# Single transposes and value products placed between the tile products of an attention head

## The chip, the cores and the metric

The kernel runs on one core of one Trainium2 chip. The metric is the time of one execution in microseconds (us) on the device. TensorE (PE) does the matrix products and the transposes, ScalarE (ACT) and VectorE (DVE) the elementwise work, and DMA queues move data between HBM and SBUF. A matrix product needs its weights loaded first; the profile shows these loads as an engine row of their own, PEld.

## The reference

One step of a two-layer encoder trunk on 512 prompt rows and 8 x 16 sample rows, 640 rows in all, model width 1024:

```
for each layer:
  q, k, v (differential attention) | q, k, v (sliding window) | two gates = x @ w_in
  for each of 8 heads, both maps m:  p_m = softmax(q_m k_m^T)        # chunk-causal
      a = p_0 - lambda * p_1 ;  o = a @ v                            # prompt rows: 4 blocks of 128
      samples: the same over 512 cached rows and the 16 new ones
      o = o * rsqrt(mean(o^2) + eps) * g
  x = LayerNorm(ALPHA * x + (sig(g_a) * (A @ w_a) + sig(g_b) * (B @ w_b)) @ w_o)
  x = LayerNorm(ALPHA * x + relu(x @ w_up)^2 @ w_down)
```

## The kernel before

All engines run programs written out by hand, in order, tied by semaphores. The large products are made in a split form: each operand is a high and a low part, and a block of 128 input rows (k = 0 to 7) takes three PE products, high by high, high by low, low by high (L602, L603, L604 in `feature_tile`). One product has 128x128 weights and moves 320 columns. A tile (128 output rows, one half of the 640 columns) is 8 x 3 = 24 such products. Below they are called tile products and numbered 0 to 23 within a tile.

Head h of the attention runs among the tiles that make q and k of head h+1. PE's order in `head(l, h)` is:

1. tile(0,0), q of the next head, first half. At k = 6 stands `mean_squares` of the head before (L873).
2. `unit_product(3)` of the head before (L867), then the scores of the samples (L745, L754, L755).
3. tile(0,1), then the masks (L822) and the scores of units 0 to 2 (L842). A unit is a block of 128 prompt rows; unit i sees i+1 blocks of keys. The masks overwrite the banks of the sample scores, so the first four wait until ACT has taken the exponentials of sample group 0, and the last two for those of group 1 (L1322, semaphore `dec_exp`).
4. `output_transposes` of the head before (L762, four), then tile(1,0), k of the next head, with `dec_transposes` of sample groups 0 and 1 (L777, five each) at k = 2 and k = 5. Both groups write the same place in PSUM: group 1 waits until ACT has copied group 0 out (L1330, `dec_t_copied`).
5. `dec_products` (L787 for the new rows, L795 for the cached ones), `last_score` (L831, L833), `unit_transpose((0, 1))` (L856, three).
6. tile(1,1), with `dec_map_sum` (L805) at k = 4 and `unit_product((0, 1))` and `unit_transpose((2,))` at k = 5. Behind it `unit_product((2,))` and `unit_transpose((3,))`. A unit's product waits until ACT has copied its transposed probabilities out of PSUM (L1314, `unit_t_copied`).

A product of two full-precision operands (L867, L787, L805, L873, L745, L795) is two PE instructions, a transpose (L762, L777, L856, L1013) is one. L795 works in strips: the weights are 32 columns wide and four strips of the array run together.

ACT's order at the end of a head is: `unit_copy(1)`, `head_swap` (L1256, four), `unit_copy(2)`, the square `d_sq` (L1443, which `mean_squares` multiplies), and `high(1)` (L1229), which makes the high part of a weight chunk. DVE then makes the low part (`low(1)`, L2113), and behind that in its queue stands `dec_mean_squares` (L2181). ACT's next head begins with `dec_rsqrts` (L1343, L1345), which waits for L2181; behind it stand `head_swap` (L1256), `output_squares` (L1350) and `dec_exps` (L1322). DVE stands between the last two: L2186 and L2188 after the squares, then the maxima of the sample scores (L2227).

In the last head of a layer gate tiles stand in place of the next head's tiles. `last_head_end` begins with a tile whose banks ACT must have copied out in `gate_copy(1)` (L1373, `gate_copied`); in front of that copy stand `unit_copy(1)` and `a_high(3)` (L1388) in ACT's queue.

Outside the heads the change touches `first_tiles` (transposes of the last block of rows, L1013, which wait for DVE's L2628), and ACT's `branch_pair`.

Of the kernel before, what the change touches and what calls it, by code (L numbers as in the profile page):

```python
# [25 lines left out]
P = 128  # L26
# [6 lines left out]
RT = ROWS // P  # L33
# [3 lines left out]
HEADS = 8  # L37
# [3 lines left out]
BANK = 512  # L41
# [70 lines left out]
def build(nc, x_rows, x_cols, k_cache, v_cache, swa_kc, swa_vc, swa_k_keep, swa_v_keep, weights, cols,  # L112
# [3 lines left out]
    with ctx:  # L116
# [470 lines left out]
        def _(pe):  # L587
            mm = nc.tensor.matmul

            def feature_tile(s, n, hi, lo, which, part=None, between=None, slot=None, order=None):  # L590
                slot = s if slot is None else slot
                if order is None:
                    order = [(half, k) for half in ((0, 1) if part is None else (part,)) for k in range(KT)]
                if part != 1:
                    pe.wait_ge(w_ready[s], n + 1)
                for half, k in order:
                    out = PS[:, bank_of(which, half), 0:HALF]
                    c = slice(half * HALF, (half + 1) * HALF)
                    if between and (half, k) in between:
                        between[half, k]()  # L600
                    wh, wl = w_hi[slot][:, k * P:(k + 1) * P], w_lo[slot][:, k * P:(k + 1) * P]
                    mm(out, wh, hi[:, k, c], start=(k == 0), stop=False)  # L602
                    mm(out, wh, lo[:, k, c], start=False, stop=False)  # L603
                    last = mm(out, wl, hi[:, k, c], start=False, stop=(k == KT - 1))  # L604
                    if k == KT - 1:
                        last.then_inc((chunk_half_done if half == 0 else chunk_done)[s], 1)

            def x_blocks():
# [147 lines left out]

            def output_transposes(l, h, bank):

                n = l * HEADS + h
                pe.wait_ge(o_n_ready, n + 1)  # L760
                for i in range(4):
                    last = nc.tensor.transpose(PS[:, bank, i * P:(i + 1) * P], o_n[:, i, :], ident[:])  # L762
                last.then_inc(o_t_ready, 1)

            def dec_transposes(l, h, g):
                n = l * HEADS + h
                pe.wait_ge(dec_exp, 2 * n + g + 1)
                if g == 0:

                    pe.wait_ge(unit_t_copied, 3 * n)  # L770
                else:
                    pe.wait_ge(dec_t_copied, 2 * n + 1)
                for t in range(5):
                    if (g, t) == (0, 4):

                        pe.wait_ge(a_done, n)
                    last = nc.tensor.transpose(flat[:, 6 * BANK + t * P:6 * BANK + (t + 1) * P],  # L777
                                               d_p[:, g, t * P:(t + 1) * P], ident[:])
                last.then_inc(dec_t_ready, 1)

            def dec_products(l, h):

                n = l * HEADS + h
                pe.wait_ge(unit_exp, 4 * n + 2)
                for g in range(2):
                    pe.wait_ge(dec_t_copied, 2 * n + g + 1)
                    mm(PS[:, g, 0:P], d_pt[:, g, 4, :], rows[:, RT - 1, bass.ts(h, P)], start=True, stop=False,  # L787
                       skip_group_check=True)
                pe.wait_ge(vc_loaded, 16 * (n + 1))
                for g in range(2):  # L790
                    for t in range(4):
                        for b in range(4):
                            rows_of = slice(32 * b, 32 * (b + 1))
                            e = slice((4 * g + b) * P, (4 * g + b + 1) * P)
                            last = mm(PS[rows_of, g, 0:P], d_pt[:, g, t, rows_of], vc[:, t, e],  # L795
                                      start=False, stop=(t == 3), skip_group_check=True)
                    last.then_inc(dec_pv, 1)

            def dec_map_sum(l, h):

                n = l * HEADS + h
                pe.wait_ge(dec_o_copied, 2 * n + 2)
                pe.wait_ge(dec_sel_ready, n + 1)
                for g in range(2):
                    last = mm(PS[:, 0, g * 64:(g + 1) * 64], d_o[:, g, :], sel_r[:, g, :], start=True, stop=True)  # L805
                last.then_inc(dec_ot_ready, 1)

# [37 lines left out]

            def unit_transpose(l, h, units):
                n = l * HEADS + h
                pe.wait_ge(unit_probs, 4 * n + units[-1] + 1)
                if units[0] == 0:
                    pe.wait_ge(dec_t_copied, 2 * n + 2)  # L850
                else:
                    pe.wait_ge(unit_t_copied, 3 * n + units[0] - 1)
                at_col = 0
                for i in units:
                    for j in range(i + 1):
                        last = nc.tensor.transpose(PS[:, 6, at_col:at_col + P],  # L856
                                                   u_a_of[i][:, j * P:(j + 1) * P], ident[:])
                        at_col += P
                last.then_inc(unit_t_ready, 1)

            def unit_product(l, h, units):
                n = l * HEADS + h
                pe.wait_ge(unit_t_copied, 3 * n + max(units[-1], 1))
                for i in units:
                    for j in range(i + 1):
                        t = (j if i == 0 else 1 + j) if i < 2 else j
                        last = mm(PS[:, 7, i * P:(i + 1) * P], u_at[max(i - 1, 0) % 2][:, t * P:(t + 1) * P],  # L867
                                  rows[:, j, bass.ts(h, P)], start=(j == 0), stop=(j == i))
                last.then_inc(unit_pv, 1)

            def mean_squares(n):
                pe.wait_ge(dec_sq_ready, n + 1)
                mm(PS[:, 1, 0:P], ones[:], d_sq[:], start=True, stop=True).then_inc(dec_ms_ready, 1)  # L873

            def head(l, h, p, first, more, uses):

                n = l * HEADS + h

                def tile(is_k, half, between=None):
                    if more:  # L880
                        head_tile(l, h + 1, is_k, half, between)
                    else:
                        early_gate(l, is_k, half, between)

                tile(0, 0, None if first else {(0, 6): lambda: mean_squares(n - 1)})
                if not first:
                    unit_product(l, h - 1, (3,))
                else:
                    for r in range(RT):
# [12 lines left out]
                unit_score(l, h, p, (2,))  # L902
                if not first:
                    output_transposes(l, h - 1, 7)
                tile(1, 0, {(0, 2): lambda: dec_transposes(l, h, 0), (0, 5): lambda: dec_transposes(l, h, 1)})
                dec_products(l, h)
                last_score(l, h, p)
                unit_transpose(l, h, (0, 1))
                tile(1, 1, {(1, 4): lambda: dec_map_sum(l, h),
                            (1, 5): lambda: (unit_product(l, h, (0, 1)), unit_transpose(l, h, (2,)))})  # L910
                unit_product(l, h, (2,))
                unit_transpose(l, h, (3,))

            def last_head_end(l):
                early_gate(l, 2, 0, {(0, 6): lambda: mean_squares(l * HEADS + HEADS - 1)})
                unit_product(l, HEADS - 1, (3,))
                early_gate(l, 2, 1)
# [103 lines left out]
            def first_tiles(l, which, n):  # L1021

                group = l * GROUPS + 4 if which else l * GROUPS
                for half in range(2):
# [8 lines left out]
                    if half == 0:  # L1033
                        for r in range(3, RT):
                            pe.wait_ge(row_evacuated[r], group)
                    feature_tile(1, n, xt_hi, xt_lo, 1, half, slot=NEXT[1],
                                 between={(0, 3): lambda: x_transposes(l, which, 4, 0),
                                          (0, 5): lambda: x_transposes(l, which, 4, 1)})

# [25 lines left out]
            for l in range(DEPTH):  # L1065
# [11 lines left out]
                for u in range(FF_PAIRS):  # L1077
# [140 lines left out]
        def _(act):  # L1218
# [173 lines left out]
            def head(l, h, p, first, more, uses):  # L1392
# [43 lines left out]
                else:  # L1436
# [51 lines left out]
            def branch_pair(l, u):  # L1488
# [1701 lines left out]
```

## Time and profile before

| what | us |
|---|---|
| median of three runs | 2154.99 (2154.5 to 2155.03) |
| the profiled execution, its own time | 2154.7 |
| its span, first to last instruction | 2152.9 |
| PE busy | 2142.3 |
| PEld busy | 1961.0 |
| DVE busy | 1470.4 |
| ACT busy | 1182.9 |

PE is pipelined: the record of a tile product lasts 0.31 us, but products start 0.147 us apart. A busy PE therefore says little; the distances between starts do. The granted TensorE clock is 0.999 of full speed, which is the upper level, 2.4 GHz.

### The profile page before, as it was taken

The numbers are of one execution on the slowest core, as the hardware profiler recorded it, in microseconds if no ns is written. First come the engines' busy times: TensorE is split into PE (matmuls) and PEld (weight loads), VectorE is DVE, ScalarE is ACT, GpSimd is POOL, SyncE is SP. The second block draws the span as 40 slices with busy tenths as digits, with TensorE's granted clock in tenths as the row PEclk, the third lists the DMA queues.
The fourth block names the chain that finished last, engine by engine and source line by source line (L and its number), as shares of the span: only waits on it lengthen the run. The fifth ranks groups of instructions, "written<-read, shape, count | busy, mean of one in ns | idle before, by whom it ended". The sixth has DMA issues, their size and how long they took to land.

```text
span 2152.9 us, 38502 instructions
## 1 busy us (share of the span) xinstructions
PE 2142.3 (100%) x15174; PEld 1961.0 (91%) x15174; DVE 1470.4 (68%) x2420; ACT 1182.9 (55%) x2513; POOL 0.2 (0%) x4
## 2 busy tenths in 40 slices
PE   9999999999999999999999999999999999999998
PEld 8998889999989898989889888899999898989897
DVE  6757777776979373636667577786768793646466
ACT  4457776686535362626234677766865262627261
POOL 0000000000000000000000000000000000000000
PEclk9999999999999999999999999999999999999999
DMA  5367562531351222222333765525113412222231
GB/s 183 104 252 257 206 227 89 156 110 51 97 173 40 92 85 79 89 69 89 108 108 103 273 247 201 203 87 178 70 60 104 156 52 86 89 69 89 75 111 69
DMA packets 68162, 268.19 MB, mean 125 GB/s; under 512 B 10984, under 2 KB 12648, under 8 KB 61296
## 3 DMA queue, kind: packets, MB, share of 16 engines
q1 hardware_dynamic: 43136, 152.75, 20.9%
q10 hardware_dynamic: 24848, 112.99, 14.8%
q8 instruction: 121, 1.98, 0.4%
q14 instruction: 57, 0.47, 0.1%
HBM read 236.35 MB, written 25.95 MB: 122 GB/s over the span
## 4 chain that ended last, share of the span: by engine, by line
PE 97%; DVE 2%; issue 0%; ACT 0%; DMA 0%; DVEq 0%; ACTq 0%
PE PS L706 10%; PE PS L705 10%; PE PS L704 10%; PE PS L636 9%; PE PS L634 9%; PE PS L635 9%; PE PS L602 9%; PE PS L603 9%; PE PS L604 9%; PE PS L867 2%; PE PS L745 1%; PE PS L795 1%; PE PS L842 1%; PE PS L978 1%; PE PS L856 1%; PE PS L958 1%
## 5 line engine op out<-in xcount | busy, mean ns | idle before, releaser
L2113 DVE TENSOR_TENSOR w_lo<-w_raw,w_hi 128x1024 fp32r<-128x1024 f32 x178 | 216.0, 1223 | 243.3 <-ACT w_hi L1229 236.1
L602 PE MATMUL PS<-xt_hi,w_hi 128*128 128x320 f32 x1184 | 380.7, 322 | 0.0
L604 PE MATMUL PS<-xt_hi,w_lo 128*128 128x320 f32 x1184 | 365.7, 309 | 0.0
L603 PE MATMUL PS<-xt_lo,w_hi 128*128 128x320 f32 x1184 | 365.5, 309 | 0.0
L1229 ACT ACTIVATE w_hi<-w_raw 128x1024 fp32r<-128x1024 f32 x178 | 186.6, 1059 | 304.6 <-PE PS L706 284.2
L704 PE MATMUL PS<-w_hi,act_a_hi 128*128 128x512 f32 x800 | 312.2, 390 | 0.0
L706 PE MATMUL PS<-w_hi,act_a_lo 128*128 128x512 f32 x800 | 311.4, 389 | 0.0
L705 PE MATMUL PS<-w_lo,act_a_hi 128*128 128x512 f32 x800 | 311.4, 389 | 0.0
L602 PEld LDWEIGHTS PS<-xt_hi,w_hi 128*128 128x128 f32 x1184 | 222.7, 188 | 3.0 <-issue 1.4
L603 PEld LDWEIGHTS PS<-xt_lo,w_hi 128*128 128x128 f32 x1184 | 223.0, 188 | 0.1
L604 PEld LDWEIGHTS PS<-xt_hi,w_lo 128*128 128x128 f32 x1184 | 222.2, 188 | 0.0
L1256 ACT ACTIVATE rope_s<-PS 32x320 f32<-32x320 f32 x352 | 151.0, 429 | 55.5 <-DVE z_all L2104 27.9
L706 PEld LDWEIGHTS PS<-w_hi,act_a_lo 128*128 128x128 f32 x800 | 150.1, 188 | 31.3
L704 PEld LDWEIGHTS PS<-w_hi,act_a_hi 128*128 128x128 f32 x800 | 150.2, 188 | 30.9 <-issue 0.5
L705 PEld LDWEIGHTS PS<-w_lo,act_a_hi 128*128 128x128 f32 x800 | 150.2, 188 | 30.7
L2730 DVE TENSOR_TENSOR part_lo<-w_raw,part_hi 128x512 fp32r<-128x512 f32 x144 | 98.0, 688 | 56.8 <-ACT part_hi L1733 53.8
L1733 ACT ACTIVATE w_hi<-w_raw 128x512 fp32r<-128x512 f32 x130 | 78.6, 623 | 61.1 <-PE PS L706 48.8
L1733 ACT ACTIVATE part_hi<-w_raw 128x512 fp32r<-128x512 f32 x144 | 88.4, 623 | 30.2 <-DVE w_raw L2716 29.1
L634 PE MATMUL PS<-t_hi,part_hi 128*128 128x320 f32 x328 | 101.4, 309 | 0.0
L635 PE MATMUL PS<-t_lo,part_hi 128*128 128x320 f32 x328 | 101.4, 309 | 0.0
L636 PE MATMUL PS<-t_hi,part_lo 128*128 128x320 f32 x328 | 101.4, 309 | 0.0
L1764 ACT ACTIVATE PS<-PS 128x320 f32<-128x320 f32 x144 | 61.0, 424 | 70.4 <-PE PS L636 70.1
(342 smaller groups left out, 4794.2 us busy)
## 6 DMA issues: line engine op xcount, KB each, us to landing
w_raw<-in_weights SPq DMA_DIRECT2D x274, 512.0 KB, 3.5
kc<-in_k_cache ACTq DMA_DIRECT2D x32, 1024.0 KB, 8.0
vc<-in_v_cache ACTq DMA_DIRECT2D x16, 2048.0 KB, 8.9
gates_kept<-a_t ACTq DMA_DIRECT2D x8, 640.0 KB, 6.7
k_out<-k_t ACTq DMA_DIRECT2D x16, 320.0 KB, 2.4
v_out<-rows ACTq DMA_DIRECT2D x2, 2560.0 KB, 17.4
mix_a<-a_t ACTq DMA_DIRECT2D x2, 2560.0 KB, 12.6
rope_c<-gates_kept ACTq DMA_DIRECT2D x10, 320.0 KB, 3.1
```

Of the source, the lines that this page charges most:

```text
L602: mm(out, wh, hi[:, k, c], start=(k == 0), stop=False)
L603: mm(out, wh, lo[:, k, c], start=False, stop=False)
L604: last = mm(out, wl, hi[:, k, c], start=False, stop=(k == KT - 1))
L634: mm(up_bank(x), wh, moving[0][:, k], start=first and k == 0, stop=False, skip_group_check=True)
L635: mm(up_bank(x), wh, moving[1][:, k], start=False, stop=False, skip_group_check=True)
L636: last = mm(up_bank(x), wl, moving[0][:, k], start=False, stop=(k == KH - 1), skip_group_check=True)
L704: mm(out, xh, wh, start=(k == 0), stop=False)
L705: mm(out, xh, wl, start=False, stop=False)
L706: last = mm(out, xl, wh, start=False, stop=(k == KT - 1))
L1229: fn(w_hi[slot][:], raw[:, j, :], ACT.Copy).then_inc(w_hi_made[s], 1)
L1733: fn(parts_of(part)[0][part_place(n, o)][:], part_source(part, n, o), ACT.Copy) .then_inc(part_hi_made if o < 5 else w_hi_made[o - 5], 1)
L2113: v.tensor_tensor(w_lo[slot][:], raw[:, raw_of(s, n)[0], :], w_hi[slot][:].bitcast(F32), ALU.subtract)\
```

## The change

In the heads, groups of transposes and 128-column products are taken apart. A helper `spread(half, first, count, one)` puts one of them in front of each of `count` tile products in a row, beginning with number `first`. The new-row products of the samples become strips like the cached ones. ACT takes `d_sq` before `unit_copy(2)`. In `branch_pair`, for u = 0, `up_seed(2)` comes before the high part number 3. In `first_tiles` the transposes move from k = 3 and 5 to k = 4 and 6.

```
     if between and (half, k, 0) in between: between[half, k, 0]()
     mm(out, wh, hi[:, k, c], ...)          # likewise (half, k, 1), (half, k, 2) before the next two
+def spread(half, first, count, one):
+    return {(half, (first + x) // 3, (first + x) % 3): (lambda x=x: one(x)) for x in range(count)}
...
 def dec_products(l, h):
     pe.wait_ge(unit_exp, 4 * n + 2)
+    pe.wait_ge(vc_loaded, 16 * (n + 1))
     for g in range(2):
         pe.wait_ge(dec_t_copied, 2 * n + g + 1)
-        mm(PS[:, g, 0:P], d_pt[:, g, 4, :], rows[:, RT - 1, bass.ts(h, P)], start=True, stop=False,
-           skip_group_check=True)
-    pe.wait_ge(vc_loaded, 16 * (n + 1))
-    for g in range(2):
-        for t in range(4):
+        for t in range(5):
             for b in range(4):
...
+                values = vc[:, t, e] if t < 4 else rows[:, RT - 1, bass.ts(h, P)]
+                last = mm(PS[rows_of, g, 0:P], d_pt[:, g, t, rows_of], values,
+                          start=(t == 0), stop=(t == 4), skip_group_check=True)
...
+def head_end(l, h):
+    return {**spread(0, 0, 3, lambda x: unit_product(l, h, 2, x)),
+            **spread(0, 8, 4, lambda x: unit_transpose(l, h, 3, x)),
+            (0, 6): lambda: mean_squares(l * HEADS + h),
+            **spread(0, 20, 4, lambda x: unit_product(l, h, 3, x))}
 def head(l, h, p, first, more, uses):
-    tile(0, 0, None if first else {(0, 6): lambda: mean_squares(n - 1)})
-    if not first:
-        unit_product(l, h - 1, (3,))
-    else:
+    tile(0, 0, None if first else head_end(l, h - 1))
+    if first:
...
-    if not first:
-        output_transposes(l, h - 1, 7)
-    tile(1, 0, {(0, 2): lambda: dec_transposes(l, h, 0), (0, 5): lambda: dec_transposes(l, h, 1)})
+    tile(1, 0, {**({} if first else spread(0, 0, 4, lambda i: output_transpose(l, h - 1, 7, i))),
+                **spread(0, 6, 5, lambda t: dec_transpose(l, h, 0, t)),
+                **spread(0, 16, 5, lambda t: dec_transpose(l, h, 1, t))})
     dec_products(l, h)
     last_score(l, h, p)
-    unit_transpose(l, h, (0, 1))
-    tile(1, 1, {(1, 4): lambda: dec_map_sum(l, h),
-                (1, 5): lambda: (unit_product(l, h, (0, 1)), unit_transpose(l, h, (2,)))})
-    unit_product(l, h, (2,))
-    unit_transpose(l, h, (3,))
+    tile(1, 1, {**spread(1, 0, 3, lambda x: unit_transpose(l, h, 1, x)),
+                **spread(1, 12, 2, lambda g: dec_map_sum(l, h, g)),
+                **spread(1, 15, 3, lambda x: unit_product(l, h, 1, x)),
+                **spread(1, 18, 3, lambda x: unit_transpose(l, h, 2, x))})
 def last_head_end(l):
-    early_gate(l, 2, 0, {(0, 6): lambda: mean_squares(l * HEADS + HEADS - 1)})
-    unit_product(l, HEADS - 1, (3,))
+    early_gate(l, 2, 0, head_end(l, HEADS - 1))
     early_gate(l, 2, 1)
...
-                 between={(0, 3): lambda: x_transposes(l, which, 4, 0),
-                          (0, 5): lambda: x_transposes(l, which, 4, 1)})
+                 between={(0, 4): lambda: x_transposes(l, which, 4, 0),
+                          (0, 6): lambda: x_transposes(l, which, 4, 1)})
...
-                 between={(0, 3): lambda: output_transposes(l, HEADS - 1, 2)})
+                 between=spread(0, 9, 4, lambda i: output_transpose(l, HEADS - 1, 2, i)))
 # ACT, end of head(l, h)
-    unit_copy(l, h, 2)
     act.wait_ge(dec_summed, n + 1)
     fn(d_sq[:], d_out[:], ACT.Square).then_inc(dec_sq_ready, 1)
+    unit_copy(l, h, 2)
     high(1, nth(l, AT_HEADS, 2) + h)
 # ACT, branch_pair(l, u)
-    if not last:
+    if 0 < u < FF_PAIRS - 1:
         part_highs(l, BRANCH, u + 1, (3,))
     up_seed(l, BRANCH, u, 2)
+    if u == 0:
+        part_highs(l, BRANCH, u + 1, (3,))
```

The waits inside the taken-apart functions stay with the first piece: the first piece of a group waits for what the group waited for.

## Rows read from the trace of the kernel before

**Rows 1.** The page: the chain that ended last, shares of the span by engine.
```profile
PE 97%; DVE 2%; issue 0%; ACT 0%; DMA 0%; DVEq 0%; ACTq 0%
```

**Rows 2.** Busy time of PE, PEld, DVE, ACT in one head, layer 0, head 3.
```profile
212.22:239.94 27.72, 27.72 (x262) 24.31 (x261) 21.15 (x51) 20.37 (x53) 0.00 (x0) 1.00 0.56 202
```

**Rows 3.** Timeline (start, length), PE: tile products 1 and 23; transposes; `mean_squares`.
```profile
214.99 0.31 PE L603 MATMUL PS<-xt_lo,w_hi 128*128 128x320 f32 x1
...
218.22 0.31 PE L604 MATMUL PS<-xt_hi,w_lo 128*128 128x320 f32 x1
...
221.51 0.71 PE L777 MATMUL PS<-ident,d_p 128*128 128x128 f32 x5
...
222.21 0.31 PE L603 MATMUL PS<-xt_lo,w_hi 128*128 128x320 f32 x1
...
237.86 0.38 PE L873 MATMUL PS<-d_sq,ones 128*128 128x128 f32 x2
...
238.23 0.30 PE L603 MATMUL PS<-xt_lo,w_hi 128*128 128x320 f32 x1
```

**Rows 4.** Timeline, weight loads (PEld) behind a group of transposes.
```profile
318.47 0.19 PEld L602 LDWEIGHTS PS<-xt_hi,w_hi 128*128 128x128 f32 x1
318.58 0.19 PEld L603 LDWEIGHTS PS<-xt_lo,w_hi 128*128 128x128 f32 x1
```

**Rows 5.** Timeline, PE: into the strips, from a tile product and from L787.
```profile
129.23 0.31 PE L604 MATMUL PS<-xt_hi,w_lo 128*128 128x320 f32 x1
129.47 0.64 PE L745 MATMUL PS<-kc,z_all 128*32 128x512 f32 x4
...
142.10 0.60 PE L787 MATMUL PS<-rows,d_pt 128*128 128x128 f32 x4
142.64 1.95 PE L795 MATMUL PS<-vc,d_pt 128*32 128x128 f32 x64
144.52 1.13 PE L831 MATMUL PS<-k_t,q_t 64*128 64x512 f32 x4
```

**Rows 6.** Timeline, all engines: transposes of samples, ACT's copies out.
```profile
223.38 0.71 PE L777 MATMUL PS<-ident,d_p 128*128 128x128 f32 x5
...
224.13 0.71 ACT L1330 ACTIVATE d_pt<-PS 128x640 f32<-128x640 f32 x1 [0.25 <-PE PS L777]
```

**Rows 7.** Timeline, ACT: `unit_copy(1)` of head 3.
```profile
233.00 0.49 ACT L1314 ACTIVATE u_at<-PS 128x384 f32<-128x384 f32 x1
```

**Rows 8.** Timeline, the chain from `high(1)` through DVE to the masks.
```profile
236.78 1.05 ACT L1229 ACTIVATE w_hi<-w_raw 128x1024 fp32r<-128x1024 f32 x1
...
237.94 1.22 DVE L2113 TENSOR_TENSOR w_lo<-w_raw,w_hi 128x1024 fp32r<-128x1024 f32 x1
239.07 0.28 DVE L2181 TENSOR_SCALAR d_ms<-PS 128x128 f32<-128x128 f32 x1
...
239.39 0.31 ACT L1343 ACTIVATE d_rs<-d_ms 128x128 f32<-128x128 f32 x1 [1.56 <-DVE d_ms L2181]
...
217.93 0.20 ACT L1322 ACTIVATION_READ_ACCUMULATOR d_p<-PS,small 128x1 f32 x1
...
218.37 0.35 PE L822 MATMUL PS<-mask_cols 128*128 128x64 bf16 x6
```

**Rows 9.** Timeline, end of the last head of layer 0, ACT and PE.
```profile
344.47 0.46 ACT L1388 ACTIVATE aq_hi<-a_t 128x320 fp32r<-128x320 f32 x1
345.40 0.70 ACT L1373 ACTIVATE rope_s<-PS 128x640 f32<-128x640 f32 x1 [0.46 <-PE PS L604]
...
346.22 0.39 PE L602 MATMUL PS<-xt_hi,w_hi 128*128 128x320 f32 x1
```

**Rows 10.** Waits of PE's queue (L856 over the run; two in the timeline).
```profile
  DVE u_a L2175: 0.7, 3
...
1082.48 0.20 PEld L1013 LDWEIGHTS PS<-ident,rows 128*128 128x128 f32 x2 [0.35 <-DVE rows L2628]
...
386.65 0.19 PEld L634 LDWEIGHTS PS<-ta_hi,w_hi 128*128 128x128 f32 x1 [0.20 <-issue]
```

More of the change, by code:

```diff
@@ L601, in feature_tile @@
                     wh, wl = w_hi[slot][:, k * P:(k + 1) * P], w_lo[slot][:, k * P:(k + 1) * P]
+                    if between and (half, k, 0) in between:
+                        between[half, k, 0]()
                     mm(out, wh, hi[:, k, c], start=(k == 0), stop=False)
+                    if between and (half, k, 1) in between:
+                        between[half, k, 1]()
                     mm(out, wh, lo[:, k, c], start=False, stop=False)
+                    if between and (half, k, 2) in between:
+                        between[half, k, 2]()
                     last = mm(out, wl, hi[:, k, c], start=False, stop=(k == KT - 1))
@@ L755, in dec_new_scores, with output_transpose, dec_transpose @@
                     mm(new, m_own_dec[:, g, :], m_negnew, start=False, stop=True).then_inc(dec_scores, 1)
-            def output_transposes(l, h, bank):
+            def output_transpose(l, h, bank, i):
                 n = l * HEADS + h
[L760 to L765, printed above, removed]
-                n = l * HEADS + h
-                pe.wait_ge(dec_exp, 2 * n + g + 1)
-                if g == 0:
-                    pe.wait_ge(unit_t_copied, 3 * n)
-                else:
[L772 to L779, printed above, removed]
+                if i == 0:
+                    pe.wait_ge(o_n_ready, n + 1)
+                last = nc.tensor.transpose(PS[:, bank, i * P:(i + 1) * P], o_n[:, i, :], ident[:])
+                if i == 3:
+                    last.then_inc(o_t_ready, 1)
+            def dec_transpose(l, h, g, t):
+                n = l * HEADS + h
+                if t == 0:
+                    pe.wait_ge(dec_exp, 2 * n + g + 1)
+                    if g == 0:
+                        pe.wait_ge(unit_t_copied, 3 * n)
+                    else:
+                        pe.wait_ge(dec_t_copied, 2 * n + 1)
+                if (g, t) == (0, 4):
+                    pe.wait_ge(a_done, n)
+                last = nc.tensor.transpose(flat[:, 6 * BANK + t * P:6 * BANK + (t + 1) * P],
+                                           d_p[:, g, t * P:(t + 1) * P], ident[:])
+                if t == 4:
+                    last.then_inc(dec_t_ready, 1)
             def dec_products(l, h):
@@ L794, in dec_products, with dec_map_sum @@
                             e = slice((4 * g + b) * P, (4 * g + b + 1) * P)
-                            last = mm(PS[rows_of, g, 0:P], d_pt[:, g, t, rows_of], vc[:, t, e],
-                                      start=False, stop=(t == 3), skip_group_check=True)
+                            values = vc[:, t, e] if t < 4 else rows[:, RT - 1, bass.ts(h, P)]
+                            last = mm(PS[rows_of, g, 0:P], d_pt[:, g, t, rows_of], values,
+                                      start=(t == 0), stop=(t == 4), skip_group_check=True)
                     last.then_inc(dec_pv, 1)
-            def dec_map_sum(l, h):
+            def dec_map_sum(l, h, g):
                 n = l * HEADS + h
[L802 to L806, printed above, removed]
+                if g == 0:
+                    pe.wait_ge(dec_o_copied, 2 * n + 2)
+                    pe.wait_ge(dec_sel_ready, n + 1)
+                last = mm(PS[:, 0, g * 64:(g + 1) * 64], d_o[:, g, :], sel_r[:, g, :], start=True, stop=True)
+                if g == 1:
+                    last.then_inc(dec_ot_ready, 1)
             def unit_at(i, m):
@@ L844, in unit_score, with unit_transpose @@
                 last.then_inc(unit_scores, 1)
-            def unit_transpose(l, h, units):
+            def unit_transpose(l, h, last_unit, x):
                 n = l * HEADS + h
[L848 to L859, printed above, removed]
@@ L861, in unit_product @@
-            def unit_product(l, h, units):
-                n = l * HEADS + h
[L863 to L869, printed above, removed]
+                i, j = ((0, 0), (1, 0), (1, 1))[x] if last_unit == 1 else (last_unit, x)
@@ new lines, in unit_transpose @@
+                if x == 0:
+                    pe.wait_ge(unit_probs, 4 * n + last_unit + 1)
+                    if last_unit == 1:
+                        pe.wait_ge(dec_t_copied, 2 * n + 2)
+                    else:
+                        pe.wait_ge(unit_t_copied, 3 * n + last_unit - 1)
+                last = nc.tensor.transpose(PS[:, 6, x * P:(x + 1) * P], u_a_of[i][:, j * P:(j + 1) * P], ident[:])
+                if (i, j) == (last_unit, last_unit):
+                    last.then_inc(unit_t_ready, 1)
@@ new lines, in unit_product @@
+            def unit_product(l, h, last_unit, x):
+                n = l * HEADS + h
+                i, j = ((0, 0), (1, 0), (1, 1))[x] if last_unit == 1 else (last_unit, x)
+                if x == 0:
+                    pe.wait_ge(unit_t_copied, 3 * n + last_unit)
+                last = mm(PS[:, 7, i * P:(i + 1) * P], u_at[(last_unit - 1) % 2][:, x * P:(x + 1) * P],
+                          rows[:, j, bass.ts(h, P)], start=(j == 0), stop=(j == i))
+                if (i, j) == (last_unit, last_unit):
+                    last.then_inc(unit_pv, 1)
@@ L873, in mean_squares @@
                 mm(PS[:, 1, 0:P], ones[:], d_sq[:], start=True, stop=True).then_inc(dec_ms_ready, 1)
+            def head_end(l, h):
[3 more added lines that the diff above has]
+                        **spread(0, 20, 4, lambda x: unit_product(l, h, 3, x))}
             def head(l, h, p, first, more, uses):
-                n = l * HEADS + h
                 def tile(is_k, half, between=None):
@@ L883, in tile @@
                         early_gate(l, is_k, half, between)
-                tile(0, 0, None if first else {(0, 6): lambda: mean_squares(n - 1)})
-                if not first:
-                    unit_product(l, h - 1, (3,))
-                else:
+                tile(0, 0, None if first else head_end(l, h - 1))
+                if first:
                     for r in range(RT):
```

## Prediction

> **What bounds the kernel.** I read the page first, then a table of one head by engine, then the timeline of PE, and last ACT and DVE beside it. The chain that ended last is 97% PE [rows 1]. In head 3, 27.72 us long, PE is never idle, while ACT and DVE have some 7 us each to spare [rows 2]. So a change pays if it takes time out of PE's own sequence, and costs if PE must wait where it now does not. Head 3's row stands for five of that view: heads 1 to 5 of layer 0 are equally long to 0.01 us, which says that no chance wait falls in them. Since records overlap, I read distances between starts. Tile products 1 and 23 start at 214.99 and 218.22: 3.23 / 22 = 0.147 us each [rows 3].
>
> **What a transpose costs, in a group and alone.** From the first of five transposes (221.51) to the tile product after next (222.21) there are 0.70 us; less one tile product, 0.553 / 5 = 0.111 us each. For `mean_squares`, two instructions, it is 238.23 - 237.86 = 0.37, less 0.147: 0.112 each [rows 3]. The cost is the same for two and for five, so there is no price per group that taking groups apart could save or add. The reason is in the weight loads. Behind a transpose the load for L602 starts at 318.47 and the next at 318.58 [rows 4]: a load takes 0.11 us and begins when the product before it begins. A lone transpose hides its own load under the 0.147 us before it, but the load of the tile product behind it still starts with the transpose and takes 0.11. I take 0.110 us alone, as in a group. The bounds: 0.107 to 0.114, since starts are rounded and tile products behind a group run up to 0.01 us closer. Some 44 instructions a head are moved: 44 x 16 x 0.003 = 2 us either way, taken as 0.
>
> The Trainium skill (TensorE: Matmul & The Clock Gate, Part 2) says that PE pulls a weight load ahead of a running product into the background buffer. The trace agrees as far as one load, not two. Were the follower's load hidden as well, the sum would be the rival "faster" below.
>
> **Strips.** L787 to L795 takes 142.64 - 142.10 = 0.54, and 0.147 before it from the last tile product. The 64 strips take 144.52 - 142.64 = 1.88, with some 0.20 to leave; so four strips take about 0.11. Afterwards: 0.24 from a tile product into strips (129.47 - 129.23) and 16 strips more, 0.44 [rows 5]. 0.69 becomes 0.68: nothing. The number of changes between strips and the full array stays the same; `unit_product(3)` before L745 is equally even.
>
> **What is moved past a wait.** Here is the cost. A transpose must be copied out by ACT before its product, and the distance between the two has shrunk. The path: the last of five transposes starts at 223.38 + 4 x 0.109 = 223.82, ACT's copy at 224.13, 0.31 later, and lasts 0.71 [rows 6]. A signal takes about 0.05: DVE's L2181 ends at 239.35, ACT's L1343 starts at 239.39 [rows 8]. Then come PE's load and its product.
>
> (a) Group 1 of the sample transposes (tile product 16) waits for the copy of group 0, whose last piece now stands before product 10. PE comes there after 0.11 + 6 x 0.147 = 0.99. The copy allows 0.31 + 0.71 + 0.05 = 1.07 plus the load, 0.06 to 0.11: a transpose's load seems the shorter, so 1.13. Wait: 0.14 us (0.08 to 0.19), in each of 16 heads: 2.2 us. Before, nine products lay between.
>
> (b) `unit_product(2)` now begins the next tile(0,0), and its transposes stand before products 18, 19, 20 of tile(1,1). Distance 0.11 + 4 x 0.147 = 0.70; needed 0.31 + 0.49 [rows 7] + 0.05 + 0.11 = 0.96. Wait: 0.26 us. In 14 heads: 3.7 us. Before, nine products lay between.
>
> (c) `unit_transpose(3)` used to end 4.8 us before the next head's scores. Now it stands before products 8 to 11 of tile(0,0). Counted back from the start of the scores, Z: 0.11, products 11 to 22 at 0.147, 0.24 for the exit, 0.22 for `mean_squares`, 0.88 for four value products: the last transpose starts at Z - 3.21. ACT copies at Z - 2.90 and, as records on ACT and DVE overlap by about 0.1 (L2113 ends at 239.16, L2181 starts at 239.07), is at `high(1)` 0.5 later, at Z - 2.41, where it was at 236.78 - 239.94 = Z - 3.16 (239.94 is the window's end [rows 2]). Taking `d_sq` first helps by 0.2, which this has in it. `high(1)` lasts 1.05, so DVE's low part starts at Z - 1.33. L2181, queued behind it, starts 1.13 later, and L1343 0.32 after that: at Z + 0.12, where it was at 239.39, Z - 0.55 [rows 8]. So 0.67 late. Behind L1343 are queued the swap, the squares, DVE's sum and maxima and both sample exponentials, with no idle time left that this does not push. In this head Z is 212.22, the window's start [rows 2]; the second exponential ended at 218.13, Z + 5.91. PE's masks start at 218.37 which is Z + 6.15, and the fifth, which waits for it, four short masks or some 0.12 later, at Z + 6.27 [rows 8]. Slack 6.27 - 5.91 - 0.05 = 0.31. Wait: 0.67 - 0.31 = 0.36 us (0.25 to 0.45). It falls in heads 1 to 6 only: the first head has no L1343, and the last no swap in that queue. 12 x 0.36 = 4.3 us.
>
> (d) End of the last head of a layer. The gate tile waits for `gate_copied`, for which ten instructions gave cover: its first product starts at 346.22, and the copy ends at 346.10 [rows 9]. Now PE goes from product 23 at time t straight to that wait. ACT takes the unit's copy (0.49 long) at t - 0.24, `a_high(3)` (0.46) at t + 0.15, and the gate copy at t + 0.51, for 0.70. With signal and load PE starts at t + 1.38, not t + 0.15: 1.2 us (0.9 to 1.3), twice: 2.5 us. It takes (b)'s place there.
>
> **What is won.** L856 waited for DVE 0.7 us over the run, in three places, 0.8 with the loads laid bare; product 8 comes over 1 us later. L1013 waited 0.35 behind L2628; 0.44 later it is free, 0.3 twice. The pair's product at 386.65 waited 0.2, 0.13 of it seen in the start [rows 10]. What is late there is the seed that `up_seed(2)` makes, queued in ACT behind a 0.62 us high part. Twice 0.13. Together 1.7 us; at least 0, at most 2.0. Giving the high part its place later uncovers nothing: its product is over 1 us off. The output transposes end 0.44 us later, and their copy 0.4; the fifth sample transpose waits for it but comes 0.6 later too.
>
> **Sum.** 2.2 + 3.7 + 4.3 + 2.5 = 12.7; less 1.7: +11.0. The profiled execution took 2154.7, 0.3 under the median. So 2154.7 + 11.0 = 2165.7, and as a median 2166.
>
> **Rivals.** Under 0.2% (4.3 us) no measurement of this kernel tells a change from none.
> "Waits covered": the copies come sooner than I count, by about a quarter microsecond, or (c) keeps its slack, and only (d) and a part remain. Against it: each distance is made of rows of the same head. Time 2154.7 - 1.7 + 2.5 + 2 = about 2157.5, and with none of the waits 2153. Chance 0.12.
> "Faster": the lone product's successor has its load hidden too, so that a lone product costs only its columns. 320 columns take 0.147, so 128 take at most 0.059; 0.05 us saved on some 36 of the moved instructions a head is 29 us: 2166 - 29 = 2137, with the waits kept. It decides the sign from 0.02 us each. For it speaks only that no single one stands alone in this trace; against it, that two and five cost the same each and that the load starts with the product before. Chance 0.04.
> "More waits": ACT and DVE, late by 0.67, meet a further wait, at the rope copies or at the ends of the layers: 0.4 us a head, 2172. Chance 0.09. That leaves 0.75 for the forecast, some of it short of one of the four waits.
>
> **Range and chances.** If (c) is absent the time is 2161.7; if (c) and (d) are, 2159. Upwards all upper ends give 2170. I take 2158 to 2171. Slower by over 0.2%: 0.84; within: 0.11; faster: 0.05.
>
> **What would show it.** Heads 1 to 6 of a layer last 28.4 to 28.6 us instead of 27.72, the first about 0.4 more than before. In the timeline the first L777 of group 1, the first product of `unit_product(2)` and the fifth mask start late by 0.14, 0.26 and 0.36; the gap before the gate tile at each layer's end is 1.2 us. A lone transpose adds 0.11 us between its two tile products. If it adds 0.06, or if the waits are absent, I am wrong.

## The result, and the profile after

| | median us | range, runs |
|---|---|---|
| before | 2154.74 | 2153.02 to 2155.03, 4 |
| after | 2168.97 | 2167.71 to 2169.62, 4 |

The ratio is 1.0069, with a 95% interval of 1.0057 to 1.0081: slower by 0.7%. The profiled execution took 2168.79 us, its span is 2167.0 us, and the granted clock is 0.999 as before. The helper adds lines, so names move: the tile products are L604, L607 and L610 (L602 to L604 before), the transposes of the samples L787 (L777), of the units L865 (L856), the unit products L874 (L867), the masks L832 (L822), the samples' old scores L755 (L745). ACT's exponentials are L1331 (L1322), its copies out L1339 (L1330) and L1323 (L1314), the gate copy L1382 (L1373).

On the page, the chain that ended last has lost some of PE's share, and two lines of ACT have entered it (compare [rows 1]):

```profile
PE 94%; ACT 3%; DVE 2%; issue 1%; DMA 0%; ACTq 0%; DVEq 0%
PE PS L714 10%; PE PS L715 10%; PE PS L716 10%; PE PS L646 9%; PE PS L645 9%; PE PS L644 9%; PE PS L604 8%; PE PS L607 8%; PE PS L610 8%; PE PS L804 2%; PE PS L874 1%; PE PS L852 1%; PE PS L987 1%; PE PS L787 1%; ACT rope_s L1265 1%; ACT d_p L1331 1%
```

The view of PE's waits names two places that were not in it before (us in total, times, the longest):

```profile
PE PS L832 <- ACT d_p L1331: 2.5, 12, 0.5
PE PS L874 <- ACT rope_s L1382: 1.9, 2, 1.0
```

Twelve times the masks, which is (c), and twice the end of a layer, which is (d). This view shows neither (a) nor (b). The view of the weight loads (PEld) has them, without a releaser, as "issue"; neither line has a counterpart in that view of the kernel before:

```profile
PEld PS L874 <- issue: 4.5, 14, 0.3
PEld PS L787 <- issue: 3.9, 16, 0.2
```

Fourteen times (b) and sixteen times (a), as forecast. Their size is read below in the distances. Of one head, by stretches (start:end length, then PE, PEld, DVE, ACT, POOL busy with counts, the clock, the DMA share, GB/s), the first head and head 4 of layer 0:

```profile
129.02:156.93 27.91, 27.81 (x269) 23.83 (x268) 18.17 (x41) 18.21 (x46) 0.00 (x0) 1.00 0.72 274
243.25:271.92 28.67, 28.37 (x273) 24.27 (x273) 21.23 (x52) 20.50 (x52) 0.00 (x0) 1.00 0.55 196
```

Head 4 answers to [rows 2]: 28.67 us, not 27.72. DVE and ACT have the same work to within 0.13 us, and PE, which was never idle, now is for 0.30; the rest of the 0.95 lies inside records that last longer. All heads 1 to 6 of both layers take 28.67 to 28.68 except head 2 of layer 0 (28.95), and the first head of each layer 27.91 instead of 27.32.

Now the four places, in the timeline of PE (start, length). To price a wait I go from one tile product with nothing beside it to the next such one, because the record of the product behind a piece begins up to 0.09 us early.

Wait (a), sample group 1 before product 16:

```profile
254.79 0.31 PE L604 MATMUL PS<-xt_hi,w_hi 128*128 128x320 f32 x1
255.12 0.30 PE L787 MATMUL PS<-ident,d_p 128*128 128x128 f32 x1
...
256.44 0.31 PE L604 MATMUL PS<-xt_hi,w_hi 128*128 128x320 f32 x1
```

From product 15 to product 21 there are 1.65 us. Six tile products of 0.147 and five transposes of 0.113 make 1.45. The wait is 0.20. All engines at this place show why:

```profile
253.96 0.27 PE L787 MATMUL PS<-ident,d_p 128*128 128x128 f32 x1
...
254.26 0.71 ACT L1339 ACTIVATE d_pt<-PS 128x640 f32<-128x640 f32 x1
...
255.09 0.14 PEld L787 LDWEIGHTS PS<-ident,d_p 128*128 128x128 f32 x1 [0.25 <-issue]
```

The last transpose of group 0 starts at 253.96, ACT's copy 0.30 later and ends at 254.97, and the load of group 1 begins 0.12 behind that end. The forecast had 0.05 there.

Wait (b), the product of unit 2 in front of the next tile:

```profile
265.06 0.27 PE L865 MATMUL PS<-ident,u_a 128*128 128x128 f32 x1
...
265.37 0.49 ACT L1323 ACTIVATE u_at<-PS 128x384 f32<-128x384 f32 x1 [1.12 <-PE PS L865]
...
265.61 0.30 PE L610 MATMUL PS<-xt_hi,w_lo 128*128 128x320 f32 x1
265.97 0.30 PEld L874 LDWEIGHTS PS<-rows,u_at 128*128 128x128 f32 x2 [0.32 <-issue]
266.00 0.46 PE L874 MATMUL PS<-rows,u_at 128*128 128x128 f32 x2
...
267.19 0.30 PE L604 MATMUL PS<-xt_hi,w_hi 128*128 128x320 f32 x1
```

From 265.61 to 267.19 there are 1.58 us; four tile products and three value products of 0.22 (twice 0.11) make 1.25. The wait is 0.33. Here too the load comes 0.11 after the copy's end (265.86).

Wait (c), the fifth mask:

```profile
248.94 0.79 ACT L1331 ACTIVATE d_p<-PS,small 128x640 f32<-128x640 f32 x1
249.39 0.29 PE L832 MATMUL PS<-mask_cols 128*128 128x64 bf16 x4
249.62 0.20 ACT L1331 ACTIVATION_READ_ACCUMULATOR d_p<-PS,small 128x1 f32 x1
249.87 0.23 PE L832 MATMUL PS<-mask_cols 128*128 128x64 bf16 x2 [0.19 <-ACT d_p L1331]
```

In [rows 8] the six masks are one run of 0.35 us. Here the fifth starts 0.48 after the first, where four short masks take 0.12: 0.36 of wait. The exponential ended 0.24 before masks began; now it ends 0.43 after.

Wait (d), the end of layer 0:

```profile
351.28 0.30 PE L610 MATMUL PS<-xt_hi,w_lo 128*128 128x320 f32 x1
351.43 0.46 ACT L1397 ACTIVATE aq_hi<-a_t 128x320 fp32r<-128x320 f32 x1
351.78 0.69 ACT L1382 ACTIVATE rope_s<-PS 128x640 f32<-128x640 f32 x1
352.53 0.49 PE L874 MATMUL PS<-rows,u_at 128*128 128x128 f32 x2 [0.95 <-ACT rope_s L1382]
...
353.75 0.30 PE L604 MATMUL PS<-xt_hi,w_hi 128*128 128x320 f32 x1
```

2.47 us between clean tile products, of which 1.25 is work as in (b): 1.22 of wait. ACT goes through unit copy, `a_high(3)` and gate copy in the forecast's order.

### The profile page after: what moved, and what is told of

The parts are those of the page before. It is cut to its first block, busy times and chain, and to the rows that moved or that the text cites. A ratio compares the mean times of both kernels' runs of the same rounds, so it can differ in the third digit from the quotient of the medians.

```text
span 2167.0 us, 38912 instructions
## 1 busy us (share of the span) xinstructions
PE 2150.7 (99%) x15366; PEld 1959.9 (90%) x15366; DVE 1471.0 (68%) x2420; ACT 1184.0 (55%) x2513; POOL 0.2 (0%) x4
## 4 chain that ended last, share of the span: by engine, by line
PE 94%; ACT 3%; DVE 2%; issue 1%; DMA 0%; ACTq 0%; DVEq 0%
PE PS L714 10%; PE PS L715 10%; PE PS L716 10%; PE PS L646 9%; PE PS L645 9%; PE PS L644 9%; PE PS L604 8%; PE PS L607 8%; PE PS L610 8%; PE PS L804 2%; PE PS L874 1%; PE PS L852 1%; PE PS L987 1%; PE PS L787 1%; ACT rope_s L1265 1%; ACT d_p L1331 1%
## 5 line engine op out<-in xcount | busy, mean ns | idle before, releaser
L604 PE MATMUL PS<-xt_hi,w_hi 128*128 128x320 f32 x1184 | 387.8, 328 | 0.0
L607 PE MATMUL PS<-xt_lo,w_hi 128*128 128x320 f32 x1184 | 381.9, 323 | 0.0
L610 PE MATMUL PS<-xt_hi,w_lo 128*128 128x320 f32 x1184 | 381.6, 322 | 0.0
L604 PEld LDWEIGHTS PS<-xt_hi,w_hi 128*128 128x128 f32 x1184 | 224.3, 189 | 3.4 <-issue 1.4
L607 PEld LDWEIGHTS PS<-xt_lo,w_hi 128*128 128x128 f32 x1184 | 223.4, 189 | 0.1
L610 PEld LDWEIGHTS PS<-xt_hi,w_lo 128*128 128x128 f32 x1184 | 222.8, 188 | 0.2
```

## The experiments

Each kernel was timed beside the kernel before. The kernels ran on several chips, so times are compared by the ratio to the kernel before on the same chip. The beginning of a run varies: the first old scores start between 127.70 and 129.63 us in kernels that are the same up to there. That is as much as some of the effects sought. So I also read from each trace the stretch from the first old scores (head 0, layer 0) to the last (head 7, layer 1), which leaves out this start and the end of layer 1.

| kernel | median us | ratio to before, 95% | stretch us | head 0 | head 4 |
|---|---|---|---|---|---|
| before | 2153.3 to 2154.7 | | 1264.70 | 27.32 | 27.71 |
| after | 2168.97 | 1.0069 [1.0057, 1.0081] | 1278.07 | 27.91 | 28.67 |
| no_a | 2164.82 | 1.0052 [1.0039, 1.0064] | 1275.01 | 27.72 | 28.48 |
| no_b | 2162.38 | 1.0041 [1.0028, 1.0053] | 1272.98 | 27.57 | 28.33 |
| no_c | 2164.33 | 1.0046 [1.0032, 1.006] | 1273.51 | 27.93 | 28.32 |
| no_d | 2167.15 | 1.0059 [1.0047, 1.0072] | 1277.07 | 27.92 | 28.68 |
| no_waits | 2154.14 | 0.9999 [0.999, 1.0008] | 1265.28 | 27.40 | 27.79 |
| no_waits_grouped | 2153.15 | 0.9993 [0.9984, 1.0002] | 1263.64 | 27.33 | 27.72 |
| grouped | 2155.77 | 1.0007 [0.9998, 1.0015] | 1265.28 | 27.35 | 27.75 |
| act_order | 2171.94 | 1.0081 [1.0067, 1.0095] | 1281.04 | 28.05 | 28.88 |
| one_wait | 2167.93 | 1.0062 [1.0048, 1.0076] | 1277.32 | 27.85 | 28.63 |
| strips | 2154.13 | 0.9999 [0.9991, 1.0008] | 1264.84 | 27.31 | 27.71 |
| grouped_x | 2153.05 | 0.9992 [0.9983, 1.0] | 1263.53 | 27.33 | 27.72 |

The theory: four new waits on short distances cost nearly all of it, and a lone piece costs as much as one in a group. Its rivals: lone pieces themselves are dear, in which case repairing the distances one by one would give back little; and the waits are one chain, in which case repairing one would give back more than its share or nothing.

### One wait taken away at a time

`no_a` moves sample group 1 two products later:

```
-spread(0, 16, 5, lambda t: dec_transpose(l, h, 1, t))
+spread(0, 18, 5, lambda t: dec_transpose(l, h, 1, t))
```

> The changed kernel, with the transposes of sample group 1 before tile products 18 to 22 instead of 16 to 20. Theory (four waits, each with its own place): the copy of group 0 is then out in time, the first L787 of group 1 no longer starts late, and 16 x 0.20 us go: 3.2 us under the changed kernel, about 2165.8. Rival (the lost time is the price of lone products, or a wait only moves on to the next one): the same 2169 within 1 us, with the wait found at the strips.

`no_b` exchanges two groups in tile(1,1), so that the last transposes stand three products further from their product:

```
-**spread(1, 15, 3, lambda x: unit_product(l, h, 1, x)),
-**spread(1, 18, 3, lambda x: unit_transpose(l, h, 2, x))
+**spread(1, 18, 3, lambda x: unit_product(l, h, 1, x)),
+**spread(1, 15, 3, lambda x: unit_transpose(l, h, 2, x))
```

> The changed kernel, with the transposes of unit 2 before products 15 to 17 of tile(1,1) and the products of units 0 and 1 before 18 to 20, so that unit 2's copy has three products more. Theory: the first product of unit_product(2) no longer waits in 14 heads, 14 x 0.33 = 4.6 us less, about 2164.4; the wait at the gate tile stays. Rival: no change within 1 us.

`no_c` puts the transposes of unit 3 before products 3 to 6 of tile(0,0), so that ACT comes sooner to `high(1)`:

```
-**spread(0, 8, 4, lambda x: unit_transpose(l, h, 3, x)),
+**spread(0, 3, 4, lambda x: unit_transpose(l, h, 3, x)),
```

> The changed kernel, with the transposes of unit 3 before products 3 to 6 of tile(0,0) instead of 8 to 11: 0.73 us earlier. Theory (the chain ACT high, DVE low, mean squares, rsqrt, swap, maxima, exponentials hangs on these transposes): the fifth mask no longer waits in heads 1 to 6, 12 x 0.35 = 4.2 us less, about 2164.8. Rival (the exponentials are late for another reason, for instance the longer tiles themselves): the fifth mask still waits 0.3 us, time unchanged within 1 us.

`no_d` gives the end of a layer its old order for two groups:

```
-early_gate(l, 2, 0, head_end(l, HEADS - 1))
+for x in range(3): unit_product(l, HEADS - 1, 2, x)
+for x in range(4): unit_transpose(l, HEADS - 1, 3, x)
+early_gate(l, 2, 0, {(0, 6): mean_squares, **spread(0, 20, 4, unit_product 3)})
```

> The changed kernel, with unit_product(2) and unit_transpose(3) of the last head of each layer ahead of the wait for gate_copied, in groups, as in the kernel before. Theory: 2 x 1.2 us less, about 2166.5. Rival: gate tile waits for something else behind the copy, under 0.5 us less.

Head 4 by stretches, first of `no_a`, then `no_b`, then `no_c`:

```profile
241.24:269.72 28.48, 28.20 (x273) 24.32 (x272) 21.24 (x52) 20.54 (x52) 0.00 (x0) 1.00 0.56 197
```

```profile
240.52:268.85 28.33, 28.11 (x273) 24.23 (x273) 21.24 (x52) 20.53 (x52) 0.00 (x0) 1.00 0.56 198
```

```profile
242.04:270.36 28.32, 28.21 (x273) 24.24 (x273) 21.23 (x51) 20.53 (x53) 0.00 (x0) 1.00 0.56 198
```

Against 28.67 each edit gives back the wait at its own place: 0.19, 0.34 and 0.35, beside 0.20, 0.33 and 0.36 read in the timeline of after. Head 0, which has no (c), gains 0.19 and 0.34 in the first two and nothing in the third (27.93). In `no_c` head 2 of layer 0 falls from 28.95 to 28.32 too, so its extra 0.27 was the same wait at the masks, grown longer. The timeline of `no_c` (head 4) shows the masks as one run again:

```profile
248.18 0.35 PE L832 MATMUL PS<-mask_cols 128*128 128x64 bf16 x6
```

`no_d` leaves the heads alone. From head 7 of layer 0 to the first head of layer 1 it takes 876.81 us instead of 877.85, 1.04 less, and about the same again at the end of layer 1: 2.0, where 2.4 was on offer. This rests on the trace: the intervals of the two ratios overlap. The waits are thus four, and each goes when its own distance is mended. In the heads they add up: 0.19 + 0.34 + 0.35 = 0.88, and head 4 of `no_waits` below is 0.88 shorter than in after. At a layer's end they do not quite: `no_a` and `no_b` shorten the way from head 7 to the next layer too, by 0.22 and 0.21.

### All four away, pieces alone and in groups

`no_waits` makes the four edits together. `no_waits_grouped` makes them too and lets the helper put a whole group in front of its first tile product:

```
-return {(half, (first + x) // 3, (first + x) % 3): (lambda x=x: one(x)) for x in range(count)}
+return {(half, first // 3, first % 3): lambda: [one(x) for x in range(count)]}
```

> All four shifts together, everything else as in the changed kernel, all pieces still alone. Theory: 14.4 us less than the changed kernel, 2154.5, equal to the kernel before; what is left is about +1.3 us for the lone pieces (0.08 us a head) against -1.5 us for the removed waits outside. Rival (a lone piece's successor has its load hidden, so being alone does pay once nothing waits): below 2145. Rival (waits move on): above 2160.

> As the run with all four shifts, but each group stands whole before its first tile product. Theory: 0.08 us a head less than with lone pieces, 1.3 us, about 2153.2; in the timeline a lone transpose adds 0.114 us and one of a group of five 0.110. Rival (lone is cheaper): this one is slower than the lone one by over 3 us.

Head 4 of `no_waits`, then of `no_waits_grouped`:

```profile
240.09:267.89 27.80, 27.80 (x274) 24.27 (x273) 21.25 (x51) 20.43 (x53) 0.00 (x0) 1.00 0.57 202
```

```profile
240.17:267.89 27.72, 27.72 (x274) 24.16 (x273) 21.24 (x51) 20.38 (x53) 0.00 (x0) 1.00 0.56 202
```

PE is never idle in either. The whole price of standing alone is 0.08 us a head, 1.3 us over 16 heads; by the medians of the same chip, 1.0 us, which the intervals of the two ratios do not tell from nothing. Their stretches differ by 1.64. About 0.5 of that is one wait outside the heads, in the trace of `no_waits` and not in that of `no_waits_grouped`; `no_a` has one like it in layer 1. What it waits for is not settled:

```profile
433.99 0.39 PE L604 MATMUL PS<-xt_hi,w_hi 128*128 128x320 f32 x1 [0.27 <-issue]
```

One can see the price of standing alone in single pieces. In after, lone transposes start 0.26 apart with a tile product between each two:

```profile
252.92 0.27 PE L787 MATMUL PS<-ident,d_p 128*128 128x128 f32 x1
252.94 0.40 PE L604 MATMUL PS<-xt_hi,w_hi 128*128 128x320 f32 x1
253.18 0.27 PE L787 MATMUL PS<-ident,d_p 128*128 128x128 f32 x1
...
253.70 0.27 PE L787 MATMUL PS<-ident,d_p 128*128 128x128 f32 x1
```

From the first to the fourth 0.78 / 3 = 0.26, less 0.147: 0.113. The group in `no_waits_grouped`:

```profile
249.32 0.31 PE L610 MATMUL PS<-xt_hi,w_lo 128*128 128x320 f32 x1
249.46 0.71 PE L787 MATMUL PS<-ident,d_p 128*128 128x128 f32 x5
...
250.16 0.31 PE L607 MATMUL PS<-xt_lo,w_hi 128*128 128x320 f32 x1
```

0.84, less two tile products: 0.546 / 5 = 0.109. So taking a group apart saves nothing and costs 0.003 to 0.004 for each piece.

Why a piece costs 0.11 either way is less settled than that it does. In the Trainium skill (TensorE: Matmul & The Clock Gate, Part 2), PE pulls weight loads ahead of the running product. In the trace of after this reaches one load deep: the record of each load begins with the product before it (lone transposes at 252.92 and 253.18), not earlier.

```profile
252.92 0.19 PEld L604 LDWEIGHTS PS<-xt_hi,w_hi 128*128 128x128 f32 x1
253.18 0.19 PEld L607 LDWEIGHTS PS<-xt_lo,w_hi 128*128 128x128 f32 x1
```

That the load sets a price of 0.11 is what products of few columns suggest. The map sums of before move only 64 columns each, and from the first of four to the tile product after next there are 231.51 - 230.92 = 0.59; less one tile product, 0.111 each:

```profile
230.92 0.55 PE L805 MATMUL PS<-sel_r,d_o 128*128 128x64 f32 x4
231.51 0.31 PE L603 MATMUL PS<-xt_lo,w_hi 128*128 128x320 f32 x1
```

But 128 full-precision columns cost about as much by themselves. Two rounds of the sample scores of before, 512 such columns each, start 0.43 apart, 0.84 ns a column, where a tile product moves a column in 0.147 / 320 = 0.46 ns:

```profile
129.92 0.61 PE L745 MATMUL PS<-kc,z_all 128*32 128x512 f32 x4
130.35 0.61 PE L745 MATMUL PS<-kc,z_all 128*32 128x512 f32 x4
```

At that rate 128 columns take 0.107 us (an estimate for the value products; that a transpose moves its columns at this rate is not shown). With 128 columns the two limits fall together, and no run here tells them apart. So a follower whose load was wholly hidden might gain nothing either.

### The same change in groups

`grouped` is after with only the helper's line changed as above; every group stands whole at its first place.

> The changed kernel, with every piece of a group before the group's first tile product, at the places of the change. Theory: the last transpose of each group then stands two to four products earlier, 0.3 to 0.6 us, which takes away the wait of sample group 1 (0.20) and most of unit_product(2) (0.33 to under 0.1) and of the masks (0.35 to under 0.1); the gate wait stays at about 0.9 us: about 2157. Rival (the late places and not the lone pieces make the waits): within 3 us of 2169.

2155.77 us, ratio 1.0007, and head 4 in 27.75 us:

```profile
239.79:267.54 27.75, 27.75 (x273) 24.17 (x273) 21.25 (x51) 20.47 (x52) 0.00 (x0) 1.00 0.56 202
```

Waits (a), (b) and (c) are gone from it although no group was moved. Of the four, only the gate tile's is left in the view of PE's waits:

```profile
PE PS L874 <- ACT rope_s L1382: 1.6, 2, 0.8
```

One wait too short for that view is left at the masks of head 2 of layer 0, which takes 27.97 us: its six masks take 0.56, not 0.35.

```profile
190.22 0.56 PE L832 MATMUL PS<-mask_cols 128*128 128x64 bf16 x6
```

This is the clearest run of the study. A group whose last piece stands two to four tile products behind its first is finished 0.3 to 0.6 us later, and whatever the group feeds has that much less time. The first pieces stand at the same places in both kernels, so it is this lateness of the last pieces, and not the new places as such, that brought the three waits of the heads.

### ACT's order, and what a second wait costs

`act_order` is after with ACT's old order at the end of a head:

```
+unit_copy(l, h, 2)
 act.wait_ge(dec_summed, n + 1)
 fn(d_sq[:], d_out[:], ACT.Square).then_inc(dec_sq_ready, 1)
-unit_copy(l, h, 2)
```

> The changed kernel, with ACT's unit_copy(2) ahead of d_sq, as in the kernel before. Theory: mean_squares then waits for a square that stands behind the late copy, 0.1 to 0.2 us a head, and high(1) comes 0.1 us sooner or later: 2 to 3 us slower than the changed kernel, about 2171.5. Rival (this reorder is itself a cause of the late masks): faster than the changed kernel.

Head 4 takes 28.88 us, 0.21 more than in after, and the waits at the masks grow from 2.5 to 3.5 us:

```profile
PE PS L832 <- ACT d_p L1331: 3.5, 12, 0.5
```

That is 0.08 a head. The other 0.12 is in front of `mean_squares`: the square is ready at 270.95, and the load of its product starts at 271.00. So the small reorder in the change is worth its 0.2 a head in this order of PE.

`one_wait` looks into the 0.12 us between the copy's end and the load in (a). The first transpose of group 1 has two waits in front of it. This kernel takes the one that is long satisfied before product 14:

```
-pe.wait_ge(dec_exp, 2 * n + g + 1)
+if g == 0: pe.wait_ge(dec_exp, 2 * n + g + 1)
...
+(0, 4, 2): lambda: pe.wait_ge(dec_exp, 2 * (l * HEADS + h) + 2)
```

> The changed kernel, with PE's wait for the exponentials of sample group 1 taken four products earlier, before product 14, where it is long fulfilled; the first L787 of group 1 then has only the wait for the copy of group 0 in front of it. Theory (two waits in front of one instruction are taken one after the other and the second costs about 0.06 us more after its signal): the load follows the end of the copy by 0.05 us instead of 0.11, the wait (a) falls from 0.20 to 0.14 us, 16 x 0.06 = 1 us less than the changed kernel, about 2168. Rival (0.11 us is what a copy's signal needs there): load 0.11 behind the copy, time the same.

```profile
253.53 0.71 ACT L1341 ACTIVATE d_pt<-PS 128x640 f32<-128x640 f32 x1
...
254.28 0.14 PEld L788 LDWEIGHTS PS<-ident,d_p 128*128 128x128 f32 x1 [0.18 <-ACT d_pt L1341]
```

The copy ends at 254.24 and the load starts 0.04 later, not 0.12. Head 4 shortens to 28.63 and head 0 to 27.85. The view also names the releaser now (`ACT d_pt`), where it said "issue". Of the 0.08 that the load gains, 0.05 reach the next tile products. In (b) the tile's own wait for its weights stands ahead of the one for the copy, which would explain the 0.11 there too; that was not tried.

### The small parts

`strips` is before with only the new rows' products as strips.

> The kernel before, with only the new rows' products made as strips. Theory: the head is shorter by 0.01 to 0.02 us, time unchanged, 2154.5 to 2154.9. Rival (sixteen more strips cost more than four full products, or the wait for the second group's copy moves behind the first group's strips and pays): over 1 us to either side.

2154.13 against 2154.62 us, and a stretch of 1264.84 against 1264.70: nothing, as costed.

`grouped_x` is `no_waits_grouped` with the transposes of `first_tiles` at their old places where they serve the feed-forward part. There the new places gain about 0.3 us in layer 1 and cost 0.14 behind them in each layer:

```
-between={(0, 4): ..., (0, 6): ...}
+between={(0, 3 if which else 4): ..., (0, 5 if which else 6): ...}
```

> As the grouped run without waits, and the transposes of the last block of rows back at k = 3 and 5 where they serve the feed-forward part (which = 1), at k = 4 and 6 only at the start of layer 1. Theory: the moved ones made DVE's sums late and cost 0.14 us behind them in each layer and won 0.3 us in layer 1 only; so within 0.3 us of the grouped run, about 2153.2, and the best of all. Rival: a difference over 1 us.

2153.05 us, 0.1 below `no_waits_grouped`, which is within the scatter. Both have a ratio of 0.9992 to 0.9993, with intervals that end at 1.0 and 1.0002: perhaps 1.5 us under the kernel before, less than this measurement settles. It would be the 0.8 of L856's waits, the 0.4 of the seed's and the 0.3 that is left of L1013's.

## Why the prediction was right

Forecast 2166.0, measured 2168.97. The four waits stood where they were forecast and as often; their terms were somewhat small, so that heads 1 to 6 took 28.67 us, just above the forecast 28.4 to 28.6. The price of a lone piece came out as forecast, but the reason given for it is not shown.

**Lone pieces.** Forecast 0.110 us, as in a group, with up to 2 us either way left open. Measured 0.113 against 0.109: 1.3 us over the run. The outcome of the rival "Faster" is ruled out by `no_waits`, in which nothing else differs from `no_waits_grouped`. Its premise fails even if the load is hidden, for the value products at least: "320 columns take 0.147, so 128 take at most 0.059" takes the rate of a tile product for that of full-precision columns, which take 0.84 ns each in L745, 0.107 for 128. The forecast's own reason, that the follower waits for its load, gives the same 0.11 and was not put to a test; that both limits give it is partly luck.

**(a)** forecast 0.14, measured 0.20, 16 times: 3.2 us for 2.2. The step that was off is "a signal takes about 0.05". It came from a signal to ACT. Here the load stands behind two waits and came 0.12 after the copy.

**(b)** forecast 0.26, measured 0.33, 14 times: 4.6 for 3.7. The distance and the copy were right (0.31 and 0.49 against 265.37 - 265.06 and 0.49); the same step was short by the same 0.06.

**(c)** forecast 0.36, measured 0.36 by the timeline and 0.35 by `no_c`, 12 times, and 0.27 more once. The chain of steps through ACT and DVE held, and the slack too. The 0.27 of head 2 of layer 0 was not foreseen, but stood in the trace of before: there the second exponential of that head ends at 190.69, 0.04 behind the start of the masks, where in head 3 it ends 0.24 ahead of it.

```profile
190.49 0.20 ACT L1322 ACTIVATION_READ_ACCUMULATOR d_p<-PS,small 128x1 f32 x1
190.65 0.35 PE L822 MATMUL PS<-mask_cols 128*128 128x64 bf16 x6
```

The forecast took the slack of head 3 for all heads, because they are equally long; but equal length shows only that none of them waits, not how near each is to waiting. What makes ACT later in head 2 is not settled.

**(d)** forecast 1.2, measured 1.22, twice.

**Strips** and the seed's place: forecast 0 and 0.26. `strips` gives 0. The seed's two places gave 0.43 in the trace.

**Wins.** L856's waits (0.8) are gone in every kernel that has the new place. L1013 gave 0.34 at the boundary of the layers and 0.30 at the start of layer 1's second part, but DVE's work there is queued differently now: its low part (at 675.41, for 1.22 us) is late, and a tile product of each layer waits 0.14 for it. Net 0.3 where 0.6 was forecast. With the 0.43 of the seed the wins are 1.5, not 1.7.

**The sum** now: lone pieces 1.3, (a) 3.2, (b) 4.6, (c) 4.2 + 0.3, (d) 2.4, less 1.5, makes 14.5. The two spans differ by 14.1, and their first old scores start at 129.02 and 129.47, which is 0.45 of chance in favour of after. The medians differ by 14.2. Of the 3 us that the forecast lacked, 1.9 are the signal in (a) and (b), and 1.3 the lone pieces; the other differences nearly cancel.

"Waits covered" is wrong by the four places. "More waits" gave 2172, which is as near to the measured time as the forecast, so the time alone does not choose between them. The places do: ACT and DVE, late by 0.67, met nothing further in heads 1 to 6 save the once in head 2, and not 0.4 us in each head.

## What to carry to other kernels

In this kernel a transpose or value product of 128 columns costs 0.11 us of PE's time in a group or alone, so spreading a group buys nothing. What it does is move the group's last piece away from its first, and with it everything that waits for the group. Before spreading, add up start of last piece, copy, signals and load, and compare with the tile products left; here distances of 0.7 and 1.0 us were too short for trips from PE to ACT and back that took 1.0 and 1.2.

## What had not been expected of the hardware

- With two waits in front of one PE instruction, the second cost more time even though the first was long satisfied: 0.12 us from the end of ACT's copy to the load, and 0.04 with one wait. The view of waits called the first "issue" and named the releaser of the second.
- A transpose standing alone costs 0.113 us against 0.109 in a group, and the product behind a piece is recorded up to 0.09 us early; distances must be taken between products that have no piece beside them.
- Full-precision columns took 0.84 ns each in the sample scores, against 0.46 ns in the tile products, so 128 of them cost about what one weight load does.
- The beginning of the run varies by up to 1.9 us between executions (first old scores at 127.70 to 129.63 us) at a granted clock that reads 1.00. Stretches inside the run repeat to 0.02 us.
